# A two-block transformer on one core: where the context columns of a norm are multiplied, and where one sum of squares stands among the matmuls

## What is computed

```python
def modulate(x, shift, scale):
    return rms_norm(x) * (1.0 + scale) + shift

h_lat = modulate(x_lat, mod_l[0], mod_l[1])
h_ctx = modulate(x_ctx, mod_c[0], mod_c[1])
...
q, k, v = jnp.split(h @ w_in, [nq, 2 * nq], axis=-1)
q = rms_norm_gain(q.reshape(b, n, DIFF_HEADS, 2, DIFF_DH), q_norm_g)
k = rms_norm_gain(k.reshape(b, n, DIFF_HEADS, 2, DIFF_DH), k_norm_g)
...
ql, kl = rope_2d(ql), rope_2d(kl)
k_all = jnp.concatenate([kc, kl], axis=1)
y_lat = out(map_query_blocks(lambda qb: diff_attend(qb, k_all, v_all, lam, scale), ql))
```

## Time and profile before

| | |
|---|---|
| time, 3 runs | 2997.04, 2997.46, 3002.53 us; median 2997.46 |
| profiled execution | 2995.62 us, its span 2993.8 us |
| mean granted TensorE clock | 0.997 of full speed |
| PE busy | 2930.9 us (98%) |
| DVE, ACT, POOL busy | 1980.2, 1276.2, 31.8 us |

### The profile page before, as it was taken

The page is one execution under the profiler, slowest core; times in us unless marked ns, Lnnn a source line. Parts: engine busy times, 40 slices in busy tenths (PEclk is TensorE's granted clock), DMA queues, the critical chain, the costliest instruction groups (busy, mean ns, idle before and its releaser), DMA issues.

```text
span 2993.8 us, 45050 instructions
## 1 busy us (share of the span) xinstructions
PE 2930.9 (98%) x17758; PEld 2494.3 (83%) x17758; DVE 1980.2 (66%) x2704; ACT 1276.2 (43%) x1471; POOL 31.8 (1%) x44
## 2 busy tenths in 40 slices
PE   8999999999989999999999999999999999999998
PEld 5896887888867788988889988888888899988887
DVE  5754656766656767467657867775677477777764
ACT  5312224222144466345444634564544345435653
POOL 0000000000010000010000000000100000000000
PEclk9999999999999999999999999999999999999999
DMA  7430343444521135555545424555555544234554
GB/s 294 144 131 22 134 148 134 163 168 160 190 77 70 59 139 184 181 197 189 202 172 183 154 86 155 183 185 194 185 182 185 209 169 169 100 138 175 191 186 169
DMA packets 71594, 475.35 MB, mean 159 GB/s; under 512 B 8064, under 2 KB 8224, under 8 KB 19744
## 3 DMA queue, kind: packets, MB, share of 16 engines
q1 hardware_dynamic: 57744, 418.47, 38.9%
q10 hardware_dynamic: 11520, 41.95, 4.2%
q0 software_dynamic: 2192, 12.96, 1.1%
HBM read 472.31 MB, written 1.05 MB: 158 GB/s over the span
## 4 chain that ended last, share of the span: by engine, by line
PE 90%; DVE 5%; ACT 2%; DVEq 1%; issue 1%; ACTq 1%; DMA 0%; SPq 0%
PE ps L499 18%; PE ps L446 12%; PE ps L448 11%; PE ps L447 11%; PE ps L500 9%; PE ps L452 6%; PE ps L454 6%; PE ps L453 6%; DVE w_lo L1882 2%; PE ps L744 1%; PE ps L714 1%; ACT w_hi L1316 1%; PE ps L442 1%; PE ps L818 1%; PE ps L1206 0%
## 5 line engine op out<-in xcount | busy, mean ns | idle before, releaser
L1882 DVE TENSOR_TENSOR w_lo<-raw,w_hi 128x2048 fp32r<-128x2048 f32 x369 | 846.0, 2293 | 499.6 <-ACT w_hi L1316 498.4
L1316 ACT CAST w_hi<-raw 128x2048 fp32r<-128x2048 f32 x367 | 701.6, 1912 | 663.0 <-PE ps L448 329.5
L499 PE MATMUL ps<-l_both,w_hi 128*128 128x512 f32 x2048 | 718.6, 397 | 4.7 <-DVE small L2057 2.4
L500 PE MATMUL ps<-l_both,w_lo 128*128 128x256 f32 x2048 | 571.5, 279 | 0.0
L499 PEld LDWEIGHTS ps<-l_both,w_hi 128*128 128x128 f32 x2048 | 384.4, 188 | 101.7 <-issue 6.5
L500 PEld LDWEIGHTS ps<-l_both,w_lo 128*128 128x128 f32 x2048 | 385.8, 188 | 0.0
L446 PE MATMUL ps<-h_both,w_hi 128*128 128x512 f32 (+1 forms) x736 | 286.0, 389 | 5.1 <-DVE h_both L1943 3.5
L448 PE MATMUL ps<-h_both,w_lo 128*128 128x512 f32 (+1 forms) x736 | 280.2, 381 | 0.0
L447 PE MATMUL ps<-h_both,w_hi 128*128 128x512 f32 (+1 forms) x736 | 280.1, 381 | 0.0
L446 PE MATMUL ps<-l_both,w_hi 128*128 128x256 f32 x848 | 247.6, 292 | 2.8 <-DVE w_lo L1936 1.2
L1437 ACT COPY low_part<-ps 128x512 f32<-128x512 f32 x150 | 88.2, 588 | 368.8 <-PE ps L500 368.8
(11 more groups left out here) (465 smaller groups left out, 5042.3 us busy)
## 6 DMA issues: line engine op xcount, KB each, us to landing
raw<-in_ws SPq DMA_DIRECT2D x396, 1024.0 KB, 4.8
aT<-in_aw ACTq DMA_DIRECT2D x80, 512.0 KB, 4.3
ln_rows<-in_lnrow POOLq DMA_DIRECT2D x4, 1024.0 KB, 6.9
X<-in_xt SPq DMA_DIRECT2D x1, 2048.0 KB, 16.9
dist<-in_ret_dist POOLq DMA_DIRECT2D x1, 2048.0 KB, 13.9
relB<-in_relb POOLq DMA_DIRECT2D x2, 768.0 KB, 6.6
c_rows<-in_crow POOLq DMA_DIRECT2D x1, 1024.0 KB, 8.0
last_rows<-in_lnrow POOLq DMA_DIRECT2D x1, 1024.0 KB, 7.7
```

What stands on the lines that cost most here:

```text
L499: mm(o.rearrange("p (a b) -> p a b", b=T), w_hi[:, s % SPLIT, blk], rhs[:, :, c, :], start=c == 0, stop=False)
L500: ins = mm(o[:, 0:T], w_lo[:, raw_slot(s), blk], rhs[:, 0, c, :], start=False, stop=c == DC - 1)
L1316: nc.scalar.copy(w_hi[:, s % SPLIT], raw[:, raw_slot(s)]).then_inc(hi_done, 1)
L1882: tt(w_lo[:, raw_slot(s)], raw[:, raw_slot(s)], w_hi[:, s % SPLIT].bitcast(F32), ALU.subtract).then_inc(lo_done, 1)
```

## The change

GpSimd no longer multiplies the context columns; VectorE does, behind its latent loop and in front of its copy of q0. On TensorE, `qk_sum(0, 0)` and `turned_query(0)` move behind more products, the whole of q1 and ka0 for the first and kb0 too for the second, so that `qk_sum(0, 1)` follows one product behind the turn and not nine. ScalarE loads its table behind the first `qk_square` and no longer in front of `diff_split(2)`. VectorE copies q1 between the fourth and the fifth context rest, and mean and copy of ka0 stand in front of `diff_lo(3)`.

```diff
-            pool.wait_ge(std_ready, 4)
-            for c in range(DC):
-                nc.gpsimd.tensor_tensor(SQ_DIFF[:, c, CTX], X[:, c, CTX], rr[:, CTX], ALU.mult).then_inc(ctx_scaled, 1)
...
-            products(24)
+            products(40)
             qk_sum(0, 0)
-            products(16)
+            products(8)
             turned_query(0)
-            products(9)
+            products(1)
             qk_sum(0, 1)
             products(2)
             qk_sum(0, 2)
...
             scales(2, LAT, ada_gains(1, 0, [(slice(0, T), 1)]), h_hi[:, :, LAT], SQ_DIFF[:, :, LAT])
-            logs_and_exps()
...
             diff_split(2)
             ctx_scales()
             qk_square(0, 0)
+            logs_and_exps()
             diff_split(3)
...
                     lo_part(2, c - 2, h_lo[:, :, LAT], h_hi[:, :, LAT], SQ_DIFF[:, c - 2, LAT])
+            dve.wait_ge(std_ready, 4)
+            for c in range(DC):
+                tt(SQ_DIFF[:, c, CTX], X[:, c, CTX], rr[:, CTX], ALU.mult).then_inc(ctx_scaled, 1)
...
             take_diff("q", 0)
             diff_lo(2)
-            ctx_los(range(DC))
+            ctx_los(range(4))
             take_diff("q", 1)
+            ctx_los(range(4, DC))
+            qk_mean(0, 0)
+            take_diff("ka", 0)
             diff_lo(3)
-            qk_mean(0, 0)
             qk_scale(0, 0)
             lambdas()
-            take_diff("ka", 0)
```

## The result

The changed kernel takes 2986.03 us, the median of seven runs (2981.28 to 2987.91), where the kernel before takes 2997.46 (2993.62 to 3002.53). The ratio is 0.9961, with a 95% interval of 0.9951 to 0.9971. The forecast was 2986.4, and the time lies in its range of 2983 to 2990.5.

What follows compares the result with a forecast made beforehand. TensorE, 90% of the chain that ended last, was taken to bound the kernel. Terms -1.6 - 7.6 - 1.8 - 1.7 + 1.7 gave -11.0 us, so 2986.4 us against the median 2997.46, range 2983 to 2990.5.

Steps and rivals of the forecast that it cites:

- The latent loop: VectorE's rests for q0: without GpSimd multiplying beside them they last 0.41 us, not 0.87, so q0 ends 1.6 us sooner.
- The context multiplications: Eight more VectorE instructions behind the latent loop, 2.7 us, cost nothing while ScalarE's split of tile 2 (1.9 us) covers them.
- ka0 without margin: ka0's eight products on TensorE find their context rests just in time: 0 lost, up to 1 us held open.
- The pause and the clock: In front of `qk_sum(0, 0)`: TensorE's 7.6 us idle goes, and with it the low clock behind it, 1.8 us.
- The wait at the turn: At `turned_query(0)`: the 1.7 us wait for the scaled q0 goes, with 0.9 us of margin.
- The table load: ScalarE's load behind the square costs 1.28 us; with the skill page's added drain the turn would wait 0.5 us.
- The new wait: At `qk_sum(0, 1)`, one product behind the turn: TensorE waits for VectorE's rotation, 1.8 us lost, booked as 1.7.
- The sum: All terms over the changed place together: -11.0 us on the profiled execution's 2995.62.
- The time: Whole kernel: 2986.4 us against the median 2997.46, 0.37% less.
- VectorE is not relieved: Rival: GpSimd does not cause the 0.87 us, the eight new instructions last that long too; gain about 6, 2991.5; chance 0.07.
- the gain does not carry: Rival: a later stage that waits for weights takes the gain back, 2997 us; chance 0.07.
- The clock rival: Rival: TensorE's short pauses drop the clock to 1.2 GHz from q0 to `qk_sum(0, 2)`, net +10, 3007 us; chance 0.03.

Runs made afterwards that it cites:

- order-only kernel: The changed kernel with the context multiplications back on GpSimd, all orders as in the change; median 2988.88 us, ratio 0.9967 to the kernel before.

## Why the prediction was right, step by step

- **The latent loop**, forecast -1.6: q1 begins 11.28 us behind the first filler, 13.02 before, so -1.74. First rest 0.42 us, as forecast; the order-only kernel, where it lasts 0.87 us again, shows GpSimd as the cause.
- **The context multiplications**, forecast 0 by cover: 2.77 us for eight, ended at 866.75; the rest of tile 2 starts at 867.26, 0.16 us behind the end of its split. Nothing in TensorE waits. Multiplied twice, they cost 2 us of wait at once, so the margin was thin, as the hand-over times said.
- **ka0 without margin**, forecast 0 with up to 1 us open: 870.70 to 876.20 is 5.50 us, the bare pace, and no wait.
- **The pause and the clock**, forecast -7.6 and -1.8: no bracket at the sum and PEclk 1.00 throughout. Filling the pause gave the clock's part as 1.86. The 1.8 set a cold sum and a matmul of 256 columns against a warm sum and one of 512, which makes it about 0.1 too small.
- **The wait at the turn**, forecast -1.7 with 0.9 to spare: q0 was scaled at 881.6, the turn came at 882.54. All of that margin is VectorE's reorder: without it, 1.10 us of wait. The prediction's times hold the reorder, as q0 is scaled right behind the rest of tile 3, but give it no price of its own; it was 1.3 us.
- **The table load**, by the row 1.28 us and nothing behind it: the square ends at 875.42, the load starts at 875.44, the split follows at 876.73. The Trainium skill ("ScalarE: Activation LUTs", section "What ACT_TABLE_LOAD costs") gives, for a switch to a different set, the load and a drain of about 1380 ns. By that figure, as an estimate, q0 would have been scaled at about 883.0 and the turn at 882.54 would have waited some 0.5 us; it did not wait. But this load is no switch, which the prediction did not see: the kernel names the same set in the load before it (L1320, at 734.13 us), and no other load lies between, so no run prices a switch at this place. A switch is the load of the earlier trace rows, from the set of Ln and Exp to that of SiLU, and its 1.28 us have the next instruction 0.01 behind them: the drain that the Trainium skill gives does not show there.
- **The new wait**, forecast +1.7: the bracket is 1.61, and 885.88 - 882.54 - 1.65 = 1.69. The kernel with four products behind the turn took it out and gained 1.86.
- **The sum**: -11.0 forecast, -11.32 measured as D. The difference of 0.3 is spread over the terms, none more than about 0.15 off.
- **The time**: 2986.4 forecast, 2986.03 measured. That the two are 0.4 us apart is luck: seven more runs of the same kernel had a median of 2988.18. So is the start of `qk_sum(0, 2)` at 888.20 for a forecast of 888.2: the first filler is 0.35 us later in this execution, and as a distance from it the forecast was 0.35 us too long. What the runs bear out is the sum of the parts, read as D.

Of the rivals, that VectorE is not relieved fell by the rows of 0.42 us, and that the gain does not carry by the medians. The clock rival needed a fall in q0: TensorE's short pauses there (858.06 to 858.27 between two chunks, where the pace is 0.12) left PEclk at 1.00. But it was judged too kindly in one respect: the prediction took the new wait of 1.7 us as safe, and the runs show pauses of 1.84 to 2.04 us with the clock fallen behind them. At the new wait itself, 1.61 us in five executions, the clock stayed up each time.

## What to carry to other kernels

When an engine pauses for something cheap, look at what that thing stands behind in its own engine's list; here a square of 0.63 us stood behind a split and eight scalings that it did not need, and the cure was to give TensorE other work first. With VectorE's list put in the matching order, 1.3 us of it, that was worth 9.6 of 11.3 us. Count each hand-over against the work that covers it, the moved ones too: a turn that gets one product of cover for 3.4 us of rotation makes a new wait of the difference. Measure a term of 2 us as a distance within the trace, since the whole time of a 3 ms kernel spreads more than that from run to run. To see whether it reaches the end, look for two executions whose work behind the place takes the same time.

## What the runs showed of the hardware

- A pause of TensorE of about 2 us can cost as much again: 2.04 us in front of ka0 was followed by eight starts at 0.43 us in place of 0.23, so 1.6 us more. Pauses of 1.6 to 1.7 us left the clock up, in the place of the change in eight profiled executions and further back in all eleven. In between it goes with the execution: every kernel has three later pauses of 1.8 to 1.9 us (near 1206, 1808 and 2667 us in the changed kernel), and the clock fell right behind them in 3, 6 and 4 of the eleven, at some 1.5 us each.
- The clock can fall without such a pause. In both executions of the changed kernel it fell near 2638 us, where TensorE runs matmuls of 64 and 128 columns and its longest pause just before is 0.44 us; in the other nine it did not.

```profile
2638.00:2641.00 3.00, 3.00 (x19) 2.58 (x17) 0.00 (x0) 0.00 (x0) 0.00 (x0) 0.50 0.22 93
```

- The same matmuls can run at two paces with a PEclk of 1.00 in both. The stretch that takes 185.0 us in ten executions (1860 to 2045 in the changed kernel) took 182.3 in that of the kernel before; four others take 112.0 or 114.1, 504.1 or 507.1, 165.0 or 168.0, 174.1 or 177.1 us, each by the execution. No run shows why.
- After a pause of 7.5 us the low clock lasted for a different number of matmuls in two kernels, nine starts in one and fourteen in the other, with the same pause.
- An elementwise VectorE instruction with two operands in SBUF, 256 columns, takes 0.42 us alone and 0.87 to 0.95 beside GpSimd's of the same kind. GpSimd's last 0.91 us (median) beside it and start 0.86 apart; no run has them alone. The same eight multiplications need 6.89 us on GpSimd and 2.77 on VectorE, and cost the latent loop 1.7 us where they run beside it.
